# The picks' stage of a product-key expert layer: where its early matmuls stand, and who issues the store of its weights

## The reference, cut to what matters

```
v1, i1 = top_k(s1, 16); v2, i2 = top_k(s2, 16)          # 8 heads x 2 halves, 128 keys each
sc, ci = top_k(v1[..., :, None] + v2[..., None, :], 16)   # over the 256 sums
experts = i1[ci // 16] * 128 + i2[ci % 16]
gates = softmax(sc)
z = h2 . peer_u[experts];  y2 = sum(gelu(z) * gates * peer_v[experts])
```

## Time and the profile before

| | |
|---|---|
| median of 3 runs | 3834.5 us (3829.78 to 3834.51) |
| profiled execution, its time / its span | 3830.91 us / 3828.5 us |
| mean granted TensorE clock | 0.895 of full |
| busy shares | PE 80%, weight loads 64%, DVE 64%, ACT 33%, POOL 21% |
| picks' stage in the span | about 2471 to 2906 us |
| bytes moved | 701 MB, mean 183 GB/s |

### The profile page before, as it was taken

One profiled execution on the slowest core, in us unless ns is written; L12 is line 12 of the kernel. 1 busy time (PEld: TensorE's weight loads), 2 busy tenths in 40 slices (PEclk: granted clock), 3 DMA queues, 4 the chain that ended last, 5 costly groups with the idle time before them and its releaser, 6 DMA issues. The chain is left out here.

```text
span 3828.5 us, 45287 instructions
## 1 busy us (share of the span) xinstructions
PE 3060.7 (80%) x15491; PEld 2457.1 (64%) x15491; DVE 2435.3 (64%) x4029; ACT 1271.8 (33%) x2122; POOL 821.3 (21%) x607
## 2 busy tenths in 40 slices
PE   5989849967886899494378464877788999999995
PEld 2876736647665666241256353777788888888884
DVE  1767646545675564566733556887763777877777
ACT  2335334434552543012101012254443333333331
POOL 0001110310120012000012001365453433433331
PEclk9999979988997999696689686898889999999998
DMA  4851359943034896521000012215556888888884
GB/s 181 306 212 31 115 194 359 358 168 118 1 113 158 332 355 252 188 76 36 14 14 1 6 61 67 66 64 164 156 174 237 311 314 333 321 325 327 323 323 176
DMA packets 229526, 701.46 MB, mean 183 GB/s; under 512 B 30054, under 2 KB 109030, under 8 KB 210806
## 3 DMA queue, kind: packets, MB, share of 16 engines
q1 hardware_dynamic: 182428, 478.19, 34.6%
q0 software_dynamic: 46944, 221.27, 15.9%
HBM read 642.20 MB, written 57.18 MB: 183 GB/s over the span
## 5 line engine op out<-in xcount | busy, mean ns | idle before, releaser
L441 PE MATMUL peer_chunks_low<-peer_chunks_down_hi,peer_chunks_bent_hi 128*128 128x512 f32 x768 | 300.1, 391 | 3.6 <-DVE peer_chunks_bent_lo L2751 3.3
L443 PE MATMUL peer_chunks_low<-peer_chunks_down_hi,peer_chunks_bent_lo 128*128 128x512 f32 x768 | 301.0, 392 | 0.0
L442 PE MATMUL peer_chunks_low<-peer_chunks_down_lo,peer_chunks_bent_hi 128*128 128x512 f32 x768 | 300.8, 392 | 0.0
L1350 DVE TENSOR_TENSOR moe_blocks_gu_lo<-moe_raw,moe_blocks_gu_hi 128x2048 fp32r<-128x2048 f32 x112 | 251.6, 2287 | 76.5 <-ACT moe_blocks_gu_hi L1314 76.5
L2625 POOL DMA_INDIRECT peer_chunks_got_up<-in_peer_u_rows,peer_rows_at x128 | 199.9, 1562 | 283.6 <-DVE peer_chunks_got_up L2755 272.7
L441 PE MATMUL peer_chunks_risen<-peer_h_hi,peer_chunks_up_hi 128*128 128x384 f32 x640 | 216.2, 338 | 5.5 <-DVE peer_chunks_up_lo L2732 5.4
L443 PE MATMUL peer_chunks_risen<-peer_h_hi,peer_chunks_up_lo 128*128 128x384 f32 x640 | 215.6, 337 | 0.0
L442 PE MATMUL peer_chunks_risen<-peer_h_lo,peer_chunks_up_hi 128*128 128x384 f32 x640 | 215.1, 336 | 0.0
L1314 ACT CAST moe_blocks_gu_hi<-moe_raw 128x2048 fp32r<-128x2048 f32 x112 | 207.6, 1906 | 15.9 <-DMA moe_raw<-in_moe_gate_up 7.3
L441 PE MATMUL moe_blocks_risen<-moe_blocks_gu_hi,moe_blocks_h_hi 128*128 128x512 f32 x448 | 198.5, 443 | 12.8 <-DVE moe_blocks_gu_lo L1350 8.0
L2631 POOL DMA_INDIRECT peer_chunks_got_down<-in_peer_v,peer_rows_at x128 | 131.3, 1026 | 270.7 <-DVE mod L2767 264.3
(11 more groups left out here) (658 smaller groups left out, 8097.9 us busy)
## 6 DMA issues: line engine op xcount, KB each, us to landing
moe_raw<-in_moe_gate_up SPq DMA_DIRECT2D x32, 2048.0 KB, 9.6
hT<-in_peer_u SPq DMA_DIRECT2D x128, 512.0 KB, 6.9
hT<-in_peer_v SPq DMA_DIRECT2D x128, 512.0 KB, 5.3
fox_o<-in_side_w SPq DMA_DIRECT2D x72, 512.0 KB, 5.9
peer_w<-peer_ahead_stage SPq DMA_DIRECT2D x24, 1024.0 KB, 6.7
peer_chunks_weights<-peer_w SPq DMA_DIRECT2D x128, 192.0 KB, 5.2
moe_raw_dn<-in_moe_down SPq DMA_DIRECT2D x16, 1024.0 KB, 8.9
hT<-in_moe_down SPq DMA_DIRECT2D x16, 1024.0 KB, 7.2
```

The costliest lines, as they stand in the source:

```text
L441: nc.tensor.matmul(out, l_hi, r_hi, start=start, stop=False)
L442: nc.tensor.matmul(out, l_hi, r_lo, start=False, stop=False)
L443: return nc.tensor.matmul(out, l_lo, r_hi, start=False, stop=stop)
L1350: v.tensor_tensor(gu_lo[:, n % 2, quarter(q)], raw[:, n % GU_SLOTS, quarter(q)], gu_hi[:, n % 2, quarter(q)].bitcast(F32), ALU.subtract).t ...
```

## The change

Of each tile's 10 chunks, 6 stand beside the picks (4 ahead of the transposes, 2 behind them) and 4 beside the groups. The 4 are cut in quarters: behind each group PE does 6 of the 24 matmuls of a chunk, so that groups 0 to 3 make the first of the four, and so on. ACT bends a chunk and rounds the next, and POOL splits, behind every fourth group. The exponential stands behind the third Gelu of a tile, not the fourth.

The 8 stores of a tile's weights leave SP's queue. ACT issues all 8 in a row, behind its last copy of the tile and ahead of the Gelu of the chunk that ended with group 15. SP waits for them once, at the end of the stage.

```diff
-    AT_PICK, AT_TURN, AT_GROUPS, EXP_AT, RING, LATER, BY_ACT = 8, 2, 8, 4, 3, 3, 4
+    AT_PICK, AT_TURN, AT_GROUPS, EXP_AT, RING, LATER, BY_ACT = 6, 2, 4, 3, 3, 3, 4
+    PART = KD // AT_GROUPS
...
+        def beside_group(t, n):
+            return (t - 1) * PER_TILE + AT_PICK + n // AT_GROUPS
+
         def behind_group(t, n):
-            start = (t - 1) * PER_TILE + AT_PICK + n // AT_GROUPS
+            start = beside_group(t, n)
             return range(start, start + (n % AT_GROUPS == AT_GROUPS - 1))
...
-                def store(t, piece):
-                    keys = slice(piece * KEYS // STORES, (piece + 1) * KEYS // STORES)
-                    sp.wait_ge(kept, 2 * group(t, GROUPS_))
-                    sp.dma_start(w_dram[keys, :, (t - 1) * P:t * P].rearrange("n p t -> p n t"), stage[:, keys]).then_inc(stored, 16)
-
-                def move_and_store(steps, t):
-                    for j, m in enumerate(steps):
-                        if t > 0 and j < STORES:
-                            store(t, j)
-                        move(m)
-                    if t > 0:
-                        for piece in range(len(steps), STORES):
-                            store(t, piece)
-
                 for m in range(2):
                     load(m)
-                for t in PARTS:
-                    move_and_store(beside_pick(t), t - 1)
-                    for n in range(GROUPS_):
-                        for m in behind_group(t, n):
-                            move(m)
-                move_and_store(REST, TILES - 1)
+                for m in range(AHEAD):
+                    move(m)
+                sp.wait_ge(stored, 16 * STORES * len(PARTS))
...
-                def lift(steps):
-                    for m in steps:
+                def lift_part(m, part):
+                    if part == 0:
                         pe.wait_ge(up_split, m + 1)
                         if m >= 2:
                             pe.wait_ge(bent, m - 1)
-                        for k in range(KD):
-                            last = passes(nc, risen[:, m % 2, :DENSE], (up_hi[:, m % 2, k], up_lo[:, m % 2, k]),
-                                          (hi[:, k, P:], lo[:, k, P:]), k == 0, k == KD - 1)
+                    for k in range(part * PART, (part + 1) * PART):
+                        last = passes(nc, risen[:, m % 2, :DENSE], (up_hi[:, m % 2, k], up_lo[:, m % 2, k]),
+                                      (hi[:, k, P:], lo[:, k, P:]), k == 0, k == KD - 1)
+                    if part == AT_GROUPS - 1:
                         last.then_inc(lifted, 1)
+
+                def lift(steps):
+                    for m in steps:
+                        for part in range(AT_GROUPS):
+                            lift_part(m, part)
...
                     for n in range(GROUPS_):
                         weigh(t, n)
-                        lift(behind_group(t, n))
+                        lift_part(beside_group(t, n), n % AT_GROUPS)
...
+                def store(t):
+                    act.wait_ge(kept, 2 * group(t + 1, 0))
+                    for piece in range(STORES):
+                        keys = slice(piece * KEYS // STORES, (piece + 1) * KEYS // STORES)
+                        nc.scalar.dma_start(w_dram[keys, :, (t - 1) * P:t * P].rearrange("n p t -> p n t"), stage[:, keys]).then_inc(stored, 16)
...
                     keep(t, GROUPS_ - 1)
+                    store(t)
                     bend(behind_group(t, GROUPS_ - 1))
```

## The result

The changed kernel takes 3857.3 us in the median of 4 runs (3854.71 to 3859.87), the kernel before 3832.1 in 4 runs beside it (3826.21 to 3834.51): a ratio of 1.0068 with a 95% interval of 1.0051 to 1.0085. It is slower, by 25.2 us in the medians.

A forecast was written before the change was run, and what follows sets the result against it. DVE's beat up to the last group, then PE's chunks, bound the end; tiles of 114.9 us and 79.9 behind the last block end 14.1 us later: 3845.0, 3848.6 by the median, said 3847; range 3820 to 3864 (forecast's own 3836 to 3861).

The forecast's parts named there:

- The block: ACT held by its eight stores in a row behind a tile's last copy: 26.5 us, at the transfer engines' drain pace.
- rival 3: No block: ACT free after 3.5 us, DVE's picks end last, 25 us earlier, 3809 us; chance 0.13.
- rival 2: Stores hold ACT at a lone store's pace, 17 us; a tile takes about 108 us, total 3827; chance 0.13.
- the tail: After the last tile: the block costs PE about 28 us, freeing the loads gives back 15.
- groups: First sum to DVE free in each tile: 44 us (ends 42 and 48), against 41.6, 44.1 and 43.2 before.
- from the block's end to the copy: ACT going on after its stores to the tile's picks copied: 20.1 us.
- up to the last copy: DVE free to ACT's last copy of the tile: 5.5 us plus 1 for the quarter, 6.5.
- behind the last block: From ACT going on after tile 3's stores to the last Gelu: 17 chunks, 79.9 us.
- to the first sum: Picks copied to group 0 summed: 17.8 us, against 22.5 in tile 2 before.
- tile 1 ahead of its groups: Two splits and lifts less ahead of the transposes take about 2 us off tile 1's picks.
- Rival 1: Groups cost more: PE at half clock while held, 48 us a tile, 12 us more in all, 3859; chance 0.14.
- the exponential: Behind the third Gelu, ready about 17.5 us after ACT goes on, so DVE's picks end late but not last.

The follow-up runs named there:

- e2: Kernel before with only the eight stores moved to ACT in a row, chunks left as they stood (no quarters): 3857.7 us, ratio 1.0071.
- e4: Changed kernel with each tile's 8 MB of weights in one store on ACT instead of eight: 3816.2 us, ratio 0.9966.
- e10: Changed kernel with each tile's weights in two stores of 4 MB on ACT instead of eight: one run, 3832.4 us.
- e11: Kernel before with each tile's weights in one store, issued by SP where the first piece was: one run, 3878.0 us.
- e9: Changed kernel with one store a tile and POOL's splits inside the groups left out but for 8 columns (not usable): one run, 3800.1 us.
- e5: Kernel before's chunks (whole lifts behind groups 7 and 15, no quarters) with one store a tile on ACT: 3819.5 us, ratio 0.9972.
- e6: One store a tile on ACT, the two chunks of the groups lifted in eighths, one behind each group: 3821.6 us, ratio 0.9976.
- e7: Changed kernel with one store a tile and POOL's splits inside the groups cut in halves, one group apart: 3817.9 us, ratio 0.9964.
- e12: One store a tile on ACT, three whole lifts beside the groups and seven chunks beside the picks: 3818.6 us, ratio 0.997.

## Why the prediction was right

**The block** was the step that decided. Forecast 26.5 us from reading SP's rows as the pace at which the transfer engines drain; measured 24.5 (e2 24.6). Both other readings fell: 3.5 us (rival 3) and 17 (rival 2). e4, e10 and e11 show the mechanism. An issue is held until the DMA ahead of it on that engine is nearly through: in e10 the hold ends 13.4 us after the first issue and the shortest landing is 16.0, in e11 28.1 and 31.5. In the first block of the changed kernel it is so for each of the seven: their holds end 2.1 to 3.0 us before the store ahead lands (the last one 24.6 us after the first issue, the seventh store lands at 27.6). The seven later issues of a block take 2.8 to 3.7 us, 3.4 in the mean, not 4.0: SP issues no load meanwhile, so the stores probably have the transfer engines to themselves.

**Tile by tile.** Forecast for the stage +14.1 us, measured +23.1. The forecast had +0.4, +0.3, +3.0 for the tiles and +10.4 for the tail; measured were +1.6, +4.2, +5.7 and +11.5. The 9.0 us between the sums are a net: the three blocks came out 6.0 us under the forecast and the other terms 15.0 over it (groups 5.5, from the block's end to the copy 3.1, up to the last copy 2.4, behind the last block 2.4, to the first sum 2.1, and tile 1 ahead of its groups -0.6). That the total lies as near as 9 us is in part luck. Tile 2 term by term, forecast and measured: free to last copy 6.5 and 7.3, block 26.5 and 24.6, from there to the copy 20.1 and 21.5, to the first sum 17.8 and 18.9, groups 44 and 46.4.

- *Groups*: 137.5 in the three tiles for 132, the largest of the terms that were too small. Two more splits were counted as 2.1 us each on a one-hot; e9 shows 5.7 for the three inside a tile's groups, and the rows around group 6 show a stretched split that also delays POOL's scaling, hence PE and the ring. The range given, 42 to 48, held. Rival 1 came near the size (48, at PE's pace, with the clock down while PE is held) but has the wrong cause: e4 has no block and its groups take 46.2 as well, and e9 keeps the quarters and is at 40.5.
- *To the first sum*: that this stretch gets shorter when the stores end ahead of it was right (18.9 for 22.5); e2, with the chunks as before, has 18.9 too.
- *From the block's end to the copy*: the exponential was said to be late but not last, at 17.5 us behind the block's end. It was last: DVE went on 20.0 behind it, since ACT's third Gelu stands behind a rounding that waits 6.9 us for its load.
- *The tail*: 114.1 for 112.9, of which 82.3 lie behind the block for 79.9. The loads do give back what was forecast there.

**What should show it** was there: the eight issues and the late Gelu (2616; forecast 2608, and 8.2 us of the difference stand ahead of the stage), and PE's idle time (23.9 to 24.0 us in each of the three blocks). ACT's wait for loads fell, but to 37.1, not below 30. Less the 8.2 us, tile 3's groups end at 2812.4 and not near 2805, and the last Gelu stands at 2926.5 and not near 2917.

**Rival 3** was the right picture of one store in place of eight. It put the stage at 406.9 us (2878.4 less 2471.5); e4 measured 414.3. Of the 7.4 us between them 5.2 lie in the tail (97.2 for 6.5 + 78.5 + 7 = 92.0) and 2.2 in the tiles, where the groups took 6.7 more and the picks less. The prediction lets this picture decide below a block of about 13 us; its own terms give 43.0 - 6.5 - 20.1 = 16.4. In e10, with 13.4, DVE waits only 0.75 us for the exponential of tile 2, so its own picks do end last there.

On the rule of "Issuing engines are not separate DMA queues" in the Trainium skill's "DMA: Bandwidth & Descriptors": for a lone store it holds, 0.44 us (e4). For eight in a row the sequencer's part is 24.5 us, within 2 us of the 26.5 in which they drain by my estimate, so "usually small" does not hold here. That a transfer engine takes turns between queues (section "Queues, rings and completion order" of the same page) agrees with e4: SP's loads land while ACT's store is under way for 37 us, and ACT waits 4.4 us for the first of them.

**The time.** Forecast 3847, measured 3857.3: within the range, and 10.3 us above the forecast, of which the terms of the stage are 9.0. The ends of the range do not come out of the terms named for them: groups of -6 to +12 and a block of +4 three times would add up to 3841 to 3871, where 3836 to 3861 and 3864 stand. Left open is what sets the last 2 to 4 us, that is how much of a DMA may be in flight when the next one is taken.

**A better version** is the changed kernel with one store a tile: e4, 3816.2 us, 0.34% under the kernel before. The intervals of e5, e6, e7 and e12 overlap its own. The quarters add nothing to it that can be told; the single store does. What is left is in e9: the splits inside the groups cost 17 us of the stage.

## What to carry to other kernels

An issue of a DMA looks cheap in the profile when it stands alone; before putting several in a row on an engine that computes, look for two in a row of the same kind and read the second one's hold: here it grew to nearly the drain time of the first. Put large stores in one DMA on an engine that issues no other soon, and not ahead of loads in the loads' own queue. Cutting PE's work finer did not help where what stood in the way was the work that it brings to POOL beside DVE.

## What the runs showed of the hardware that was not expected

One DMA of 8 MB in runs of 512 bytes is handed over by ACT in 0.38 to 0.44 us (e4, three of them), as the first of two of 4 MB (e10) and the first of eight of 1 MB are, while the second of two holds the engine 12.9 us. On SP's queue, beside ACT's store, most loads are issued in 1.1 to 1.7 us (e4), and behind its landing in 0.43. On POOL a subtraction of 128x8 took 2.25 us beside DVE (e9), nearly a whole one-hot of 2.28. By the rows its price there is the wait, not its size:

```profile
2555.10 2.25 POOL L2443 TENSOR_TENSOR peer_ahead_up_lo<-hT,peer_ahead_up_hi 128x8 fp32r<-128x8 f32 x1
```

That 8 columns cause no stop of DVE and a whole split does may lie in the 2.2 us between them (4.42 less 2.25); this was only argued.
